# Output projections and norms of a two-layer block, channel-major instead of token-major

## The chip, the cores and the metric

The kernel runs on one core of one Trainium2 chip, written for its engines directly: TensorE (PE), VectorE (DVE), ScalarE (ACT), GpSimd (POOL) and the queue of SyncE (SP), each with its own instruction stream, tied by semaphores. The time is the device time of one execution in microseconds (us), the median of several.

## What is computed

All in fp32, 256 tokens of 2048 channels. A RWKV-7 mixer, a differential attention and a third block with pooling, convolution, gates and an MLP follow one another. What matters here are the three places where an output projection is normed, and the last one after the MLP:

```python
# after the RWKV mixer and after attention (w_out is 2048 x 2048)
x = layernorm(ALPHA * x + (y * silu(g)) @ w_out, ln_g[layer], ln_b[layer])
k_sh, v_sh = x @ w_k_shared, x @ w_v_shared          # after layer 0
# the third block; 16 meta rows stand before the 256 tokens
u = rms_norm(h, g_pre_mix);  proj = u @ w_in
...
h = h + rms_norm(m @ w_o, g_post_mix)
u = rms_norm(h, g_pre_mlp)
f = square(relu(u @ w_up)) @ w_down
out = h + rms_norm(f, g_post_mlp)
```

In the mixer, `y` is group-normed, a bonus term is added, and the sum is multiplied by the gate: bonus and gate wait in DRAM scratch while the scan runs.

## The kernel before

Every weight matrix goes through the core once, in groups of 512 columns. A group is eight slabs of two 128-row tiles (`wraw`, 128x1024). The queue of SP loads them into a ring of four. ScalarE rounds a slab to fp32r (`whi`, `split_hi`, L294), VectorE forms the rest (`wlo`, `split_lo`, L300), and TensorE makes three products for each pair of operands (`three`: high by high, high by low, low by high). `group_slabs` (L305) runs four slabs ahead of TensorE. A slot of the ring comes free when TensorE has used its slab (`slab_used`), so every engine keeps step with TensorE, one slab in 2.8 us.

There are two forms of a group. `ws_group` (L465) keeps a 128x128 tile of weights and streams the 256 tokens: the result has channels on partitions. `wm_group` (L484) keeps the activations and streams 512 weight columns: the result has tokens on partitions. The activations themselves (`ahi`, `alo`) always have channels on partitions.

The projections `wout`, `bout` and `wo` use `wm_group` (`wm_stage`, L718, for the first), so that a norm over the 2048 channels runs along the free axis. For `wout` and `bout`, `ln_evac` (L1477) adds the residual to each group and takes statistics. After the last group, `ln_sqrt`, `ln_norm` and `ln_dve` norm the four column blocks, multiply by the gain row and add the bias row, both spread over partitions by DMA. Then `turn` (L504) transposes the result back to channel-major on TensorE, four tiles a block, and `turned_hi` and `turned_lo` form `ahi` and `alo` for the next stage. After `bout`, the RMS norm of the third block (`squares`, `rms`, `normed_turned`) stands between LayerNorm and turn. After `wo`: `rms(1)`, `post` (gain and residual), `rms(2)`, `normed_turned`. At the end `rms(3)` and `post` work through four column blocks, and SP stores each.

Before `wout`, the last part of the scan ends with the group norm on VectorE (L1377 to L1397). TensorE turns its result (L714), ScalarE applies gain and bias (L1030), VectorE adds the bonus and multiplies by the gate (L1469, L1471), and both engines form `ahi` and `alo` (L1024, L1465). GpSimd issues the loads of gate and bonus (L425, L426) once the last scan product is done.

The order of the engines' work is written out by hand: each engine's program is one list, and hooks put extra steps after chosen slabs.

## Time and profile before

| | |
|---|---|
| median of 3 runs | 2653.46 us (2651.31 to 2658.47) |
| the profiled execution | 2655.8 us, its span 2654.0 us |
| mean granted TensorE clock | 0.967 of full speed |
| TensorE busy | 2491.5 us, 94% |
| VectorE, ScalarE, GpSimd busy | 1538.5, 1122.6, 190.2 us |
| bytes moved | 431.99 MB, mean 163 GB/s |

The profile is that of one execution. Its span runs from the first to the last instruction. "Idle before" is the time in which the engine stood still ahead of an instruction, and the name behind the arrow is what released it. The granted clock is given as a share of full speed: 1.00 is 2.4 GHz and 0.50 is 1.2 GHz. A matmul's end is modelled, so the distance from one start to the next is the better measure of its cost.

### The profile page before, as it was taken

The numbers are of one execution on the slowest core, as the hardware profiler recorded it, in microseconds if no ns is written. First come the engines' busy times: TensorE is split into PE (matmuls) and PEld (weight loads), VectorE is DVE, ScalarE is ACT, GpSimd is POOL, SyncE is SP. The second block draws the span as 40 slices with busy tenths as digits, with TensorE's granted clock in tenths as the row PEclk, the third lists the DMA queues.
The fourth block names the chain that finished last, engine by engine and source line by source line (L and its number), as shares of the span: only waits on it lengthen the run. The fifth ranks groups of instructions, "written<-read, shape, count | busy, mean of one in ns | idle before, by whom it ended". The sixth has DMA issues, their size and how long they took to land.

```text
span 2654.0 us, 51395 instructions
## 1 busy us (share of the span) xinstructions
PE 2491.5 (94%) x21592; PEld 2313.9 (87%) x21592; DVE 1538.5 (58%) x1671; ACT 1122.6 (42%) x1339; POOL 190.2 (7%) x148
## 2 busy tenths in 40 slices
PE   6889999999897999999879999999699999999997
PEld 4889998999787989998679999998599988999885
DVE  6687756654655444555657987555555544455444
ACT  3444343222334444665344434544444433444433
POOL 4053303420000000000000000000000000000000
PEclk8889999999898999999989999999799999999999
DMA  6346563230465665446555656565366666666653
GB/s 188 128 140 210 165 196 110 81 97 28 160 189 161 187 186 179 143 144 185 165 157 174 180 167 175 158 183 173 118 183 183 188 186 188 185 187 182 187 187 126
DMA packets 219285, 431.99 MB, mean 163 GB/s; under 512 B 17057, under 2 KB 21153, under 8 KB 217361
## 3 DMA queue, kind: packets, MB, share of 16 engines
q1 hardware_dynamic: 214496, 404.64, 50.9%
q0 software_dynamic: 3456, 20.51, 2.0%
q10 hardware_dynamic: 1152, 4.19, 0.4%
q8 instruction: 142, 2.33, 0.4%
q14 instruction: 39, 0.31, 0.0%
HBM read 420.91 MB, written 8.39 MB: 162 GB/s over the span
## 4 chain that ended last, share of the span: by engine, by line
PE 85%; DVE 7%; ACT 3%; POOL 2%; DMA 1%; issue 1%; SPq 0%; ACTq 0%; DVEq 0%; POOLq 0%
PE ps L459 25%; PE ps L460 25%; PE ps L461 25%; PE ps L613 6%; DVE wlo L302 2%; ACT whi L298 1%; POOL M L383 1%; POOL M L385 1%; DVE act_lo L1274 1%; PE ps L663 1%; DMA M<-gate_input_scratch 1%; DMA regions<-bonus_scratch 1%; DVE regions L1512 0%; PE ps L512 0%; DVE regions L1745 0%
## 5 line engine op out<-in xcount | busy, mean ns | idle before, releaser
L302 DVE TENSOR_TENSOR wlo<-wraw,whi 128x1024 fp32r<-128x1024 f32 x752 | 953.2, 1272 | 935.9 <-ACT whi L298 934.8
L298 ACT ACTIVATE whi<-wraw 128x1024 fp32r<-128x1024 f32 x752 | 794.9, 1059 | 1255.9 <-PE ps L461 1249.8
L459 PE MATMUL ps<-act_hi,whi 128*128 128x256 f32 (+1 forms) x3968 | 1137.5, 287 | 14.2 <-DVE wlo L302 6.4
L460 PE MATMUL ps<-act_lo,whi 128*128 128x256 f32 (+1 forms) x3968 | 1124.5, 283 | 0.0
L461 PE MATMUL ps<-act_hi,wlo 128*128 128x256 f32 (+1 forms) x3968 | 1122.9, 283 | 0.0
L459 PEld LDWEIGHTS ps<-act_hi,whi 128*128 128x128 f32 x3968 | 755.0, 190 | 19.5 <-DVE wlo L302 7.3
L460 PEld LDWEIGHTS ps<-act_lo,whi 128*128 128x128 f32 x3968 | 757.2, 191 | 0.6
L461 PEld LDWEIGHTS ps<-act_hi,wlo 128*128 128x128 f32 x3968 | 754.3, 190 | 0.0
L459 PE MATMUL ps<-whi,act_hi 128*128 128x512 f32 x512 | 205.2, 401 | 7.4 <-DVE act_lo L1598 7.4
L460 PE MATMUL ps<-wlo,act_hi 128*128 128x512 f32 x512 | 204.7, 400 | 0.0
L461 PE MATMUL ps<-whi,act_lo 128*128 128x512 f32 x512 | 203.3, 397 | 0.0
L461 PE MATMUL ps<-whi,regions_r 128*128 128x512 f32 x512 | 203.0, 396 | 0.0
L460 PE MATMUL ps<-wlo,regions_r 128*128 128x512 f32 x512 | 203.0, 396 | 0.0
L459 PE MATMUL ps<-whi,regions_r 128*128 128x512 f32 x512 | 203.0, 396 | 0.0
L459 PEld LDWEIGHTS ps<-whi,act_hi 128*128 128x128 f32 x512 | 97.4, 190 | 31.9 <-issue 7.7
L461 PEld LDWEIGHTS ps<-whi,act_lo 128*128 128x128 f32 x512 | 97.3, 190 | 23.9
L460 PEld LDWEIGHTS ps<-wlo,act_hi 128*128 128x128 f32 x512 | 97.5, 190 | 22.6
L461 PEld LDWEIGHTS ps<-whi,regions_r 128*128 128x128 f32 x512 | 96.4, 188 | 23.5
L460 PEld LDWEIGHTS ps<-wlo,regions_r 128*128 128x128 f32 x512 | 96.4, 188 | 23.4
L459 PEld LDWEIGHTS ps<-whi,regions_r 128*128 128x128 f32 x512 | 96.4, 188 | 23.4
L613 PE MATMUL ps<-regions 64*64 64x64 f32 x3072 | 103.7, 223 | 8.6 <-POOL regions L418 8.6
L613 PEld LDWEIGHTS ps<-regions 64*64 64x64 f32 x3072 | 97.2, 138 | 15.2 <-POOL regions L418 9.8
(241 smaller groups left out, 1724.9 us busy)
## 6 DMA issues: line engine op xcount, KB each, us to landing
wraw<-in_a_w_in SPq DMA_DIRECT2D x128, 512.0 KB, 4.7
wraw<-in_w_up SPq DMA_DIRECT2D x128, 512.0 KB, 3.7
wraw<-in_w_down SPq DMA_DIRECT2D x128, 512.0 KB, 4.6
wraw<-in_w_in SPq DMA_DIRECT2D x112, 512.0 KB, 3.7
wraw<-in_b_w_qg SPq DMA_DIRECT2D x64, 512.0 KB, 3.9
wraw<-in_a_w_out SPq DMA_DIRECT2D x32, 512.0 KB, 4.6
wraw<-in_w_k_shared SPq DMA_DIRECT2D x32, 512.0 KB, 4.6
wraw<-in_w_v_shared SPq DMA_DIRECT2D x32, 512.0 KB, 4.7
```

The lines of the kernel that those rows point to most:

```text
L298: nc.scalar.activation(whi[:, q % RING], wraw[:, q % RING], ACT.Copy).then_inc(hi_ready, 1)
L302: nc.vector.tensor_tensor(wlo[:, q % RING], wraw[:, q % RING], whi[:, q % RING].bitcast(F32), ALU.subtract).then_inc(lo_ready, 1)
L383: ptt(xtmp(u), xx[:, k2, :], ve(mu)[:, k2].unsqueeze(2).broadcast_to([P, 2, T]), ALU.mult).then_inc(S["xa_mul"], 1)
L385: ptt(xtmp(u), xtmp(u), xT[:, k2, :], ALU.add).then_inc(done, 1)
L459: mm(o, hi_s, hi_m, start=first, stop=False, skip_group_check=True)
L460: mm(o, hi_s, lo_m, start=False, stop=False, skip_group_check=True)
L461: i = mm(o, lo_s, hi_m, start=False, stop=last, skip_group_check=True)
L613: m_ = mm(ps[r_, o_bank, (j % 8) * N:(j % 8 + 1) * N], lhs(r_, j), rhs(r_, j), start=n_ == 0, stop=n_ == len(terms) - 1)
L663: m_ = mm(ps[hs:hs + N, b, (j % 4) * P:(j % 4 + 1) * P].rearrange("p (a t) -> p a t", a=2), Kc[hs:hs + N, j, ts], KR[hs:hs + N, j, :, ts], ...
L1274: st.do(tt(alo[:, k2, 0:T], xtmp(u), ahi[:, k2, 0:T].bitcast(F32), ALU.subtract), sig["xs_ready"])
```

## The change

The three output projections are computed with `ws_group`, channel-major, and their norms too. Sums over channels are now sums over partitions and tiles: VectorE folds the tiles of a group by adds, and products with a vector of ones finish the sum. A scale for each token is spread over the partitions as a product of ones with a diagonal matrix. The transposes ahead of the next stage go away.

- `wout`, `bout`: the first three groups are summed to a preliminary mean, which is taken off before squaring. The last group (`last_group`) is finished tile by tile, and each tile is added, squared and summed behind the next. The normed result comes in seven chunks of 1, 1, 2, 2, 2, 4 and 4 tiles of 128 channels (`norm_dve`, `norm_act`), each chunk released to TensorE when its low part is formed. In `norm_dve`'s list "x" scales and shifts a chunk, "l" forms its low part, and "s" is `split_lo` of a slab. `square_quad` waits until the fold of the square before has begun.
- After `bout`: gain and bias of LayerNorm and of the RMS norm are combined. The RMS scale itself is deferred. The first two `cv` groups use the operand without it and their results are scaled later; the third uses the scaled operand, formed beside the second.
- `wo`: gains are applied at the evacuation, and `H` is kept as it is. The second norm is deferred past the MLP: squared ReLU makes its scale a factor on the MLP's result, which goes into the last norm (`q4`). The residual is completed beside the groups of `up0`, turned to token-major there (32 transposes), and stored from `Htok`.
- The gate and bonus loads are split in 12 (`EARLY`) and 4 tiles of 16. The first part is issued after the sixth state product.
- At the end gain, scale and residual are one operation for each half block, and the stores are issued from SP and ScalarE.
- A square root of a constant is placed where it makes ScalarE load that function's table early.

The core of the diff:

```diff
+CHUNKS = ((0, 1), (1, 2), (2, 4), (4, 6), (6, 8), (8, 12), (12, 16))
 # GpSimd
-            pool.wait_ge(S["y_mm"], 8)
...
-            pool.dma_start(gT, gate_dram[:, :, :]).then_inc(S["gate_loaded"], 16)
-            pool.dma_start(bvT, bonus_dram[:, :, :]).then_inc(S["bv_loaded"], 16)
+            for part, (k0, k1) in enumerate(((0, EARLY), (EARLY, KT))):
+                if part == 0:
+                    pool.wait_ge(S["m_mm"], 6)
+                else:
+                    pool.wait_ge(S["y_mm"], 8)
+                pool.dma_start(bonus_at[part], bonus_dram[:, k0:k1, :]).then_inc(S[f"bv_loaded{part}"], 16)
+                pool.dma_start(gate_at[part], gate_dram[:, k0:k1, :]).then_inc(S[f"gate_loaded{part}"], 16)
+            pool.dma_start(xre, xT_ap[:, :, 1:T + 1]).then_inc(S["x_reloaded"], 16)
 # TensorE
-            wm_stage("wout", lambda k: XS["z"] + k // 2 + 1)
-            turn(0, XS["ln0"], H)
+            def last_group(G, xh, xl, hook, after):
+                outs = [ps[:, b, 0:T] for b in (2, 3, 6, 7)]
+                ws_group(G, [(o, True) for o in outs], T, xh, xl, hook=hook, slabs=SLABS - 2)
+                for b in range(4):
+                    for q in (SLABS - 2, SLABS - 1):
+                        for kk in range(2):
+                            three(outs[b], whi[:, q % RING, kk, c], wlo[:, q % RING, kk, c], xh[:, 2 * q + kk, 0:T],
+                                  xl[:, 2 * q + kk, 0:T], first=False, last=done,
+                                  sig=slab_used if b == 3 and kk == 1 else S["tile_mm"] if done else None)
+                    after(b)
+            def token_sums(i, centred):
+                def tile(n):
+                    if centred:
+                        pe.wait_ge(S["d_ready"], 4 * i + n + 1)
+                        for tb in range(2):
+                            mm(ps[:, 0, tb:tb + 1], block(H[:, 12 + n, :], tb), one, start=n + tb == 0, stop=n == 3, skip_group_check=True)
+                    pe.wait_ge(S["sq1_ready"], 4 * i + n + 1)
+                    for tb in range(2):
+                        mm(ps[:, 5, 2 + tb:3 + tb], block(sq1[n], tb), one, start=False, stop=n == 3, skip_group_check=True)
+                def after(b):
+                    if b == 1:
+                        pe.wait_ge(S["accq_ready"], (1, 2, 4)[i])
+                        for tb in range(2):
+                            mm(ps[:, 5, 2 + tb:3 + tb], block(accQ, tb), one, start=tb == 0, stop=False, skip_group_check=True)
+                    if b:
+                        tile(b - 1)
+                    if b == 3:
+                        tile(3)
+            def spread(i, terms):
+                for a_, term in enumerate(terms):
+                    pe.wait_ge(S["stat_dve"], BY_DVE[f"{term}{i}"])
+                    for tb in range(2):
+                        mm(block(ps[:, SPREAD[a_], :], tb), ones, dg[:, tb, a_, :], start=True, stop=True)
+            for s in range(3):
+                ws_group(G0["wout"] + s, packed(2 * (s % 2)), T, ahi, alo, (lambda k: XS["z"] + k // 2 + 1) if s == 0 else None,
+                         lnv_turn if s == 1 else None)
+            last_group(G0["wout"] + 3, ahi, alo, mean_of(0), token_sums(0, True))
+            spread(0, ("scale", "shift"))
 # ScalarE
+            def mean_hook(i):
+                def hook(u):
+                    if u == 0:
+                        act.wait_ge(S["stat_mm"], MM[f"mean{i}"])
+                        st.do(a(cmean, ps[:, 4, 0:T], ACT.Copy, scale=1.0 / (12 * P)), sig["stat_act"])
+                    if u in (1, 2, 3):
+                        act.wait_ge(S["stat_dve"], BY_DVE[f"cen{i}_{u - 1}"])
+                        square_quad(H[:, 4 * u - 4:4 * u, :])
+            def norm_act(i, nxt, affine, src_, tiles_done):
...
+                for c, (k0, k1) in enumerate(CHUNKS):
+                    act.wait_ge(S["xh_ready"], (XH["ln0"], XH["u1"], XH["u2"])[i] + c + 1)
+                    for k in range(k0, k1):
+                        if affine:
+                            affine(k)
+                    st.do(a(ahi[:, k0:k1, 0:T], src_[:, k0:k1, :], ACT.Copy), sig["n_hi"])
+                    if c >= 3:
+                        split_hi(act, nxt, c + 1)
 # VectorE
+            def add_residual(i, name, other, extra=None):
...
+                def hook(u):
+                    if u == 0:
+                        dve.wait_ge(S["stat_act"], BY_ACT[f"mean{i}"])
+                        st.do(stt(H[:, 12:16, :], other[:, 12:16, :], ALPHA, cmean.unsqueeze(1).broadcast_to([P, 4, T]), ALU.mult, ALU.subtract))
+                    if u < 3:
+                        st.do(tt(H[:, j4, :], H[:, j4, :], cmean.unsqueeze(1).broadcast_to([P, 4, T]), ALU.subtract), sig["stat_dve"])
+                    if u in (2, 3, 4):
+                        fold_squares(u - 2, 3)
+                group_slabs(dve, split_lo, G0[name] + 3, hook, slabs=6)
+                for n in range(4):
...
+                    st.do(tt(H[:, 12 + n, :], H[:, 12 + n, :], last_at[n], ALU.add), sig["d_ready"])
...
+            def norm_dve(i, nxt, scale_chunk, src_):
+                for what, n in (("x", 0), ("x", 1), ("l", 0), ("x", 2), ("l", 1), ("x", 3), ("l", 2), ("s", 2), ("l", 3), ("x", 4),
+                                ("s", 3), ("x", 5), ("l", 4), ("s", 4), ("x", 6), ("l", 5), ("s", 5), ("l", 6), ("s", 6), ("s", 7)):
...
+            for s in range(3):
+                group_slabs(dve, split_lo, G0["cv"] + s, lambda u, s=s: rms_dve(8 * s + u), start=0 if s else 4)
...
+            for c in range(4):
+                for tb in range(2):
+                    st.do(stt(Htok[:, tb, cols], yG[c][:, tb, :], rrstd[:, tb:tb + 1], Htok[:, tb, cols], ALU.mult, ALU.add), sig["out_cols"])
```

## Rows read from the trace of the kernel before

**Rows 1.** The page, part 1: busy us of each engine, share, instructions.
```profile
PE 2491.5 (94%) x21592; PEld 2313.9 (87%) x21592; DVE 1538.5 (58%) x1671; ACT 1122.6 (42%) x1339; POOL 190.2 (7%) x148
```

**Rows 2.** Waits of TensorE: line, releaser: total us, times, longest us.
```profile
PE ps L512 <- DVE regions L1631: 46.5, 6, 20.1
```

**Rows 3.** Windows: busy (x) PE, PEld, DVE, ACT, POOL; granted clock; DMA share, GB/s.
```profile
699.07:706.72 7.65, 0.00 (x1) 0.03 (x1) 3.07 (x5) 1.69 (x4) 0.00 (x0) 0.72 1.00 419
...
801.20:822.26 21.06, 7.52 (x32) 6.32 (x33) 17.54 (x20) 9.93 (x13) 2.67 (x5) 0.59 0.23 79
...
1316.30:1347.28 30.98, 6.39 (x33) 5.76 (x33) 23.43 (x30) 16.05 (x30) 1.98 (x3) 0.62 0.40 137
...
1882.60:1911.69 29.09, 7.26 (x32) 6.46 (x33) 20.92 (x28) 13.96 (x28) 0.54 (x1) 0.57 0.14 40
...
2636.90:2654.00 17.10, 0.00 (x0) 0.00 (x0) 11.82 (x15) 1.74 (x5) 0.00 (x0) 0.63 0.33 123
```

**Rows 4.** Timeline, 670 to 711: start us, us, engine, line, operation, count [idle <-releaser].
```profile
670.61 0.69 DVE L1452 TENSOR_TENSOR M<-M,ps 128x512 f32<-128x512 f32 x1 [3.25 <-PE ps L613]
...
689.24 0.58 POOL L425 DMA_DIRECT2D regions<-gate_scratch  x1 [113.98 <-PE ps L613]
...
691.34 7.73 PE L714 MATMUL ps<-cst,regions 64*64 64x64 f32 x192 [2.40 <-DVE regions L1397]
...
695.17 0.69 DVE L1397 TENSOR_TENSOR regions<-regions,small 128x512 f32<-128x512 f32 x1
...
703.58 0.69 DVE L1469 TENSOR_TENSOR regions<-regions 128x512 f32<-128x512 f32 x1 [7.72 <-DMA regions<-bonus_scratch]
...
706.72 3.68 PE L714 MATMUL ps<-cst,regions 64*64 64x64 f32 x64 [7.66 <-ACT regions L1030]
...
710.33 0.79 PE L459 MATMUL ps<-whi,act_hi 128*128 128x512 f32 x1
```

**Rows 5.** Windows, as rows 3: long and short products, starts after a pause.
```profile
710.32:801.20 90.88, 90.87 (x386) 72.81 (x384) 53.50 (x54) 38.35 (x42) 0.00 (x0) 0.99 0.56 177
...
822.25:825.39 3.14, 3.14 (x16) 3.14 (x15) 1.23 (x1) 1.03 (x1) 0.00 (x0) 0.50 0.89 363
...
1219.07:1222.76 3.69, 0.00 (x1) 0.03 (x1) 2.51 (x3) 3.58 (x4) 0.00 (x0) 0.81 0.55 157
...
1222.76:1228.10 5.34, 5.34 (x13) 4.18 (x14) 4.56 (x4) 3.68 (x4) 0.00 (x0) 0.50 0.31 96
...
2274.80:2456.76 181.96, 181.96 (x1537) 181.95 (x1536) 95.48 (x79) 80.88 (x78) 0.00 (x0) 1.00 0.63 184
```

**Rows 6.** Timeline of TensorE: small products and transposes, columns as rows 4.
```profile
128.48 1.94 PE L546 MATMUL ps<-cst,regions 128*128 128x2 f32 x16
...
1342.07 1.09 PE L512 MATMUL ps<-cst,regions 128*128 128x128 f32 x8 [1.99 <-DVE regions L1631]
...
1647.79 3.61 PE L825 MATMUL ps<-regions,cst 128*128 128x256 f32 x16
```

**Rows 7.** Groups by line and shape: count, busy us, mean ns, idle before.
```profile
L298 ACT ACTIVATE whi<-wraw 128x1024 fp32r<-128x1024 f32 x752 | 794.9, 1059 | 1255.9 <-PE ps L461 1249.8 <-DMA wraw<-in_a_w_in 6.1
...
L1493 DVE TENSOR_TENSOR act_lo<-ps,act_hi 128x1024 fp32r<-128x1024 f32 x12 | 14.7, 1221 | 10.2 <-ACT act_hi L1051 10.2
...
L1030 ACT ACTIVATE regions<-ps,vec 128x256 f32<-128x256 f32 x16 | 8.0, 555 | 0.0
...
L1566 DVE TENSOR_SCALAR regions<-regions,small 128x128 f32<-128x128 f32 x8 | 2.2, 279 | 0.0
```

**Rows 8.** Timeline: a 256-column pass and a table load, columns as rows 4.
```profile
1315.79 0.42 DVE L1615 TENSOR_TENSOR act_lo<-regions,act_hi 128x256 fp32r<-128x256 f32 x1
...
1885.97 1.28 ACT L1157 ACT_TABLE_LOAD   x1
```

**Rows 9.** Timeline of VectorE at the end, columns as rows 4.
```profile
2640.38 1.41 DVE L1745 SCALAR_TENSOR_TENSOR regions<-regions,small 128x512 f32<-128x512 f32 x2
...
2649.57 1.22 DVE L1747 TENSOR_TENSOR regions<-regions 128x1024 f32<-128x1024 f32 x1
```

More of the change, by code:

```diff
@@ L303, in split_lo, with group_slabs @@
                                     ALU.subtract).then_inc(lo_ready, 1)
-        def group_slabs(eng, split, G, hook=None, slabs=SLABS):
-            for u in range(slabs):
+        def group_slabs(eng, split, G, hook=None, slabs=SLABS, start=0):
+            for u in range(start, slabs):
                 g, q = (G, RING + u) if u < RING else (G + 1, u - RING)
@@ L517, in _ @@
+            by_chunk = lambda name: lambda k: XS[name] + chunk_of[k] + 1
             for i in range(2):
@@ new lines, in centred_tile, with tile, lnv_copy @@
+            def centred_tile(i):
+                def tile(n):
+                    act.wait_ge(S["d_ready"], 4 * i + n + 1)
+                    st.do(a(sq1[n], H[:, 12 + n, :], ACT.Square), sig["sq1_ready"])
+                return tile
+            def lnv_copy(u):
+                if u == 5:
+                    act.wait_ge(S["stat_mm"], MM["rows"])
+                    st.do(a(lnv[:, 0:80], ps[:, 6, 0:80], ACT.Copy), sig["stat_act"])
+            for s in range(3):
+                group_slabs(act, split_hi, G0["wout"] + s, lnv_copy if s == 1 else None)
@@ L1770, in _ @@
                         G = G0[f"down{half}"] + 2 * s + part
-                        group_slabs(dve, split_lo, G)
+                        group_slabs(dve, split_lo, G, gained(s - 1) if half and s and part else None)
                     dve.wait_ge(slab_used, SLABS * (G + 1))
```

616 lines of the change are left out of this document (402 added, 214 removed).

## Prediction

> **What bounds the kernel now.** I read the page's busy shares first: TensorE is busy 94% of the span, every other engine at most 58% [rows 1]. So the time is TensorE's products plus the places where TensorE waits, and a change can only pay where it waits, or cost where it lengthens its stream. Second, the list of waits for TensorE: its largest entry, 46.5 us, is the transposes at L512 waiting for VectorE [rows 2]; they stand behind each output projection. Third, the windows laid over the stretches without projection products: 7.65 us before the last turn of the scan's output, 21.06 us after `wout`, 30.98 us after `bout`, 29.09 us after `wo`, 17.10 us at the end [rows 3], 105.9 us together. The reader should see in them that VectorE and ScalarE take turns (17.5 and 9.9 us of the 21.06) while TensorE does only 32 transposes, and that the clock is at half: the first 16 products after the `wout` gap took 3.14 us where 1536 took 181.96, 0.118 each [rows 3, 5]. That start costs 3.14 - 15 x 0.118 = 1.4 us more, here and after `bout`; about 1.1 after `wo`.
>
> **Early bonus and gate loads.** VectorE ends the group norm at 695.86 and starts the output stage at 703.58, held by the load from the scratch; TensorE stands still until 706.72 and starts `wout` at 710.33 [rows 4]. The change issues three quarters of both loads after the sixth state product, seen by VectorE at 670.61 [rows 4]. Now 4 MB, issued at 689.24, are in by 703.5, so 3 MB want about 11 us and land near 682, 14 us early; the last quarter, issued where all was before, is wanted six steps of 1.9 us later. So VectorE starts at 695.9, 7.7 us earlier. TensorE's two last turns no longer follow a pause: at their earlier pace (7.73 us for six) they take 2.6 instead of 3.6 us, from 699.1, and `wout` starts at 701.7, 8.6 us earlier. The slow start of `wout` (six products at 0.43 instead of 0.233) goes too: 1.2 us. Sum 9.8; without the two clock effects 7.7.
>
> **Twelve groups turned round.** Groups of `wout`, `bout` and `wo` had 96 products of 512 columns, now 192 of 256. By the rows 384 long ones take 90.88 us, 1.2 of them the slow start, so 0.2335 each and 22.4 us a group; 1536 short ones take 0.1185 each and 22.75 us a group [rows 5]. Twelve groups cost +4.3 us. The Trainium skill speaks against this edit too: TensorE: Matmul & The Clock Gate, Back-to-back issue gap, gives each product its columns at the clock plus a fixed 2.5 ns, so twice as many products cost more. By that rule the twelve groups would cost an estimated 2.9 us instead of 4.3 and the total would be 1.4 us lower; the row decides.
>
> **New small products inside the stream.** Eight products with a two-column operand left 16 records and took 1.8 us, 0.22 each; eight fp32 products of 256 columns 3.5 us, 0.43 each; eight transposes 1.09 us [rows 6]. Added: two sums for the mean (0.9), the turn of the gain rows (0.15), the deferred RMS scale inside `cv` (two sums, two spreads, 0.9), one residual sum (0.4), 32 transposes inside `up0` (4.4). Sum +6.7 us, all on TensorE, nothing hides it. The 96 old transposes lie inside the windows above.
>
> **LayerNorm after `wout`.** I lay out the last group from its start, with these prices: 1.22 us for 1024 columns on VectorE, 0.69 for 512, 0.42 for 256, 0.28 for a 128-column scaling, 1.06 for a weight rounding and 0.55 for a 256-column scaling on ScalarE [rows 4, 7, 8]. The three old evacuations become adds and folds, hidden beside TensorE's 22.7 us. Sum for the mean at 5.7, `cmean` at 6.6. Then the queues of both engines hold one another: a square (ScalarE) waits until the fold before it has begun (VectorE), the next weight rounding stands behind that square, and VectorE's `wlo` behind that rounding. VectorE: add and first centring to 9.0, third centring 13.7, fold 14.4; ScalarE square to 15.4, rounding 16.5; `wlo` 17.7, fold 19.1; square 19.5, rounding 20.6, `wlo` 21.8, fold 23.7, `wlo` 24.9, first tile added 25.3. TensorE is through tile 1 at 20.3 and must wait for the folded squares (23.7) and the first tile (25.3); then sums 0.9, tile 2, sums, tile 3: 30.0 at full clock. So 6.9 us more than a plain group (22.66 plus 0.43 counted above). Idle of 3.69 us was followed by 5.34 us at half clock [rows 5]; the same here slows 24 products and the sums: +3.
> Tail: tile 4 added 30.5, squared 30.9, sums 31.75, variance 31.95, root 32.2, reciprocal 32.4, diagonal 33.0, spread 33.75, second diagonal and spread 34.5, first chunk scaled and shifted 34.95, gain 35.55, rounded 36.0, low part 36.45: TensorE resumes 6.45 us after its last tile.
> First `ks` group: VectorE owes per four k three passes of 1.22 and two `wlo`, 6.1 us, where TensorE wants 5.7. Walking the written order of chunks (1, 1, 2, 2, 2, 4, 4) gives TensorE stalls of 0.3, 0.7, 1.8 and 1.9 us: 4.7. A slow start is absorbed by the third.
> Before: 21.1 + 1.4 = 22.4. After: 6.9 + 3 + 6.45 + 4.7 = 21. Gain 1.4 us.
>
> **LayerNorm and RMS norm after `bout`.** The same new chain, stalls 4.0 since a `cv` product has 272 columns: 20.4. Before 31.0 + 1.4 = 32.4, because a second norm stood in line. It is now deferred: squares, folds and the scale run beside the first two `cv` groups, and the third group needs the scaled operand. VectorE and ScalarE spend about 3.1 to 3.7 us a slab there against TensorE's 3.0, and four slabs of ring cover it; cover gone, each slab costs 0.7. Gain 12.0 us.
>
> **RMS norms after `wo`.** No centring: squares and folds are done a group ahead. Inline cost 1.3 (two sums for the folds and for three tiles); tail: square 0.45, sum 0.45, root 0.35 (its table is loaded early, which hides 1.28 us [rows 8]), reciprocal and diagonal 0.75, spread 0.5, scale and add 0.95, rounding and low part 0.85, hand-overs: 4.65; stalls in the first `up0` group 4.6. Sum 10.6 against 29.1 + 1.1. Gain 19.5 us. VectorE's new residual work (two passes of 1.22 in four slots) puts it behind the second `up0` group: -0.5.
>
> **The end.** Before: last product 2636.9, VectorE's evacuation, ScalarE's two squares, root by 2640.4, then four rounds of 2.6 us to 2650.8 and 3.2 us for the last store [rows 9]. After: the gain product hides under the squares; two more tiny scalings (+0.4), then eight fused passes at 0.67: 5.4 instead of 10.4 us. Gain 4.7 us. The stores are half as large and split over two queues; I count nothing for that.
>
> **Sum.** 9.8 + 1.4 + 12.0 + 19.5 + 4.7 = 47.4, less 4.3 + 6.7 + 0.5 = 11.5: 36 us gained. The profiled execution took 2655.8 us, 1.8 of them around its span of 2654.0, and lies 2.3 above the median of 2653.46; it becomes 2619.8, and against the median 2617.5.
>
> **Bounds of what the trace does not show.** The half clock inside the last group: 0 to 4.5 us a norm. The weave's wait there: between 0 (if the squares' turn is not the one that comes last) and 10 (each of three hand-overs a further 1.1). The chunked first groups: 0 to 9 us each, for VectorE's share is within 8% of TensorE's. I take my walk through the code for each, since every step has a row.
>
> **Rivals.**
> *Leaner tails (chance 0.15).* If the engines run ahead where I let them wait, the last groups lose neither 6.9 nor the clock's 3 in two norms: 2 x 9.9 less, 2598. For: the ring holds four slabs, so a late `wlo` need not be felt. Against: the written order puts squares before roundings in one queue.
> *Dearer weave (0.16).* The hand-overs cost double in two last groups and in three first groups: +6.9 and +3 x 3.5, 2635. For: VectorE owes 6.1 us where TensorE wants 5.7. Against: short operations follow one another within 0.04 us in the rows.
> *The early loads do not help (0.04).* If another wait lies right behind the load (ScalarE's first write), 7.7 us are lost: 2625. The rows show ScalarE's write done 7 us before, so it is unlikely.
> *Slower than before (0.05): the chunk sweep runs in lockstep.* Some 20 VectorE steps a sweep each wait for a ScalarE step and that for VectorE. TensorE starves for the delay of each, in three sweeps. The 36 us are gone at 0.6 us a step; at 0.85 a step (a rounding of 512 columns and its hand-over) it costs 51 us: 2669. Against: in the written order two chunks of scaling stand between a chunk and its low part.
>
> **How the numbers follow.** The forecast case, 2617.5, has 0.60 and its own range is 2607 to 2629. With both neighbours in, 2598 to 2638 leaves out some 2 in 10. A measurement of this kernel tells about 0.3% from no change, 8 us, so "faster" is below 2645.5. Forecast, leaner, loads and nearly all of the dearer case lie there: 0.92; same 0.04, from the dearer case's end; slower 0.04.
>
> **What would show it.** Right: `wout` starts near 702; between the last `wout` product and the first of `ks` some 6.5 us, not 21; a hole of about 5 us inside that last group, ended by VectorE; holes of 1.8 and 1.9 us at the seventh and ninth k of `ks`, `cv` and `up0`; no hole in the second `cv` group; 12.4 us after the last product instead of 17.1. Wrong: many holes near 1 us in the first groups (lockstep), half clock for long stretches of them, or a wait for the RMS scale in `cv`.

## The result, and the profile after

The changed kernel takes 2632.33 us (median of 5 runs, 2629.56 to 2641.17) against 2654.44 of the kernel before on the same chip: ratio 0.9918, 95% interval 0.9897 to 0.9939. That is faster by more than 0.3%, 22 us by the medians. The profiled execution took 2629.58 us, its span is 2627.8; the spans differ by 26.2 us (2654.0 before). The forecast was 2617.5 with a gain of 36 us, so the time is 15 us above the forecast: inside the wide range of 2598 to 2638, but above 2607 to 2629, the range given for the forecast case by itself, and nearest to the 2635 of "dearer weave".

First the page, part 1 (as [rows 1]), then the waits of TensorE (as [rows 2]) from the last group of `wout` on (769 to 830) and from that of `bout` on (1280 to 1400). L492 is the first product of a triple, L574 the sum of the folded squares, L594 a spread, L894 the RMS sum in the second `cv` group.

```profile
PE 2504.4 (95%) x22809; PEld 2380.5 (91%) x22809; DVE 1576.8 (60%) x1756; ACT 1166.1 (44%) x1433; POOL 191.0 (7%) x149
```

```profile
PE ps L492 <- DVE act_lo L1756: 4.5, 3, 2.1
PE ps L574 <- DVE regions L1692: 2.9, 1, 2.9
PE ps L594 <- DVE M L1744: 1.3, 1, 1.3
```

```profile
PE ps L894 <- DVE regions L1692: 5.2, 1, 5.2
PE ps L492 <- DVE act_lo L1756: 3.5, 2, 2.1
PE ps L574 <- DVE regions L1692: 3.3, 1, 3.3
PE ps L594 <- DVE M L1744: 1.3, 1, 1.3
```

The 46.5 us at the turns are gone. What the reader is to see in their place is L1692: it is the last step of the fold of squares, and three holes of TensorE wait for it, 2.9, 3.3 and 5.2 us. For each of the first two a hole of "about 5 us" was forecast, for the third none: "no hole in the second `cv` group", and a wait there was named as a sign of being wrong.

The windows that answer to [rows 3] (columns as there): behind the last tile of `wout`, `bout` and `wo`, and behind the last product.

```profile
803.97:812.70 8.73, 5.29 (x26) 4.93 (x24) 4.27 (x16) 4.19 (x8) 1.66 (x3) 0.50 0.15 53
1320.34:1326.77 6.43, 2.97 (x24) 2.66 (x24) 4.26 (x16) 4.19 (x8) 0.00 (x0) 0.87 0.00 0
1876.14:1881.70 5.56, 2.17 (x13) 1.73 (x12) 2.73 (x9) 3.73 (x7) 0.00 (x0) 0.68 0.00 0
2615.02:2627.79 12.77, 0.00 (x0) 0.00 (x0) 8.48 (x14) 1.74 (x5) 0.00 (x0) 0.65 0.49 164
```

They were 21.06, 30.98, 29.09 and 17.10 us [rows 3]: 98.2 together, now 33.5. So 65 us of gaps went, and 26 us of time. The rest came back inside the stream, as turned groups, small products and new holes. The table says what each stretch gained. It goes by the first product of each stage in the trace's records (before: scan's last product ends 688.94, `wout` 710.33, `ks` 822.26, `vs` 914.71, `bout` 1222.76, `cv` 1347.28, gates 1493.08, `wo` 1791.31, `up0` 1911.69, `down0` 2094.89, last product ends 2636.85, after: 688.39, 701.22, 812.70, 908.33, 1216.38, 1326.77, 1483.56, 1782.09, 1881.70, 2073.05, 2615.02). The forecast is put together from the terms of the prediction for the same stretch; small products and turned groups are in it.

| stretch | before | after | gained | forecast |
|---|---|---|---|---|
| scan's end to `wout` | 21.39 | 12.83 | 8.6 | 8.6 |
| `wout` and `ks` | 204.38 | 207.11 | -2.7 | +0.6 |
| `bout`, `cv` and pool | 270.32 | 267.18 | 3.1 | 9.2 |
| `wo` and `up0` | 303.58 | 290.96 | 12.6 | 12.8 |
| the end | 17.15 | 12.78 | 4.4 | 4.7 |

The rest (start to the scan's end, `vs` to `bout`, gates to `wo`, `down0` on) gives 0.2. Three of five stretches came out within 0.3 us. The missing 9.4 us lie in two: 3.3 in `wout` and `ks`, 6.1 in `bout`, `cv` and pool.

In both, one thing is late. ScalarE in the last group of `wout` (start, duration, engine, line, operation, operands, count, idle before and its releaser); L1176 squares four tiles, L328 rounds weights:

```profile
779.33 1.06 ACT L1176 ACTIVATE regions<-regions 128x1024 f32<-128x1024 f32 x1 [1.48 <-DVE regions L1722]
780.29 1.04 ACT L328 ACTIVATE whi<-wraw 128x1024 fp32r<-128x1024 f32 x1
784.53 1.06 ACT L1176 ACTIVATE regions<-regions 128x1024 f32<-128x1024 f32 x1 [3.19 <-DVE regions L1686]
785.50 1.04 ACT L328 ACTIVATE whi<-wraw 128x1024 fp32r<-128x1024 f32 x1
788.49 1.06 ACT L1176 ACTIVATE regions<-regions 128x1024 f32<-128x1024 f32 x1 [1.95 <-DVE regions L1686]
```

The squares wait 3.19 and 1.95 us for L1686, the first step of a fold, which empties the one buffer of squares. The rounding of weights stands behind them in the queue, and VectorE waits for that (2.13 and 1.41 us ahead of its `wlo` at 786.57 and 790.54). In the first `cv` group the same ring runs, first ScalarE, then VectorE:

```profile
1352.03 2.08 ACT L1323 ACTIVATE regions<-regions,lnv 128x256 f32<-128x256 f32 x4 [1.90 <-DVE regions L1686]
1354.02 1.04 ACT L328 ACTIVATE whi<-wraw 128x1024 fp32r<-128x1024 f32 x1
1356.95 2.08 ACT L1323 ACTIVATE regions<-regions,lnv 128x256 f32<-128x256 f32 x4 [1.90 <-DVE regions L1686]
```

```profile
1355.09 1.23 DVE L332 TENSOR_TENSOR wlo<-wraw,whi 128x1024 fp32r<-128x1024 f32 x1 [3.10 <-ACT whi L328]
1356.23 0.68 DVE L1686 TENSOR_TENSOR regions<-regions 128x512 f32<-128x512 f32 x1
```

Squares 2.08, rounding 1.04, `wlo` 1.23, fold 0.68: a round takes 1356.95 - 1352.03 = 4.92 us (the steps overlap by some 0.1), in which ScalarE idles 1.90 and VectorE 2.4 to 3.4. Neither is short of time; they hand one buffer back and forth. That is the theory that the experiments test. Its rivals: VectorE's own load is what is late; TensorE merely asks too early; the ring of four weight slabs runs dry.

### The profile page after: what moved, and what is told of

Same layout as the page of the kernel before. It is cut to its first block, busy times and chain, and to the rows that moved or that the text cites. A ratio compares the mean times of both kernels' runs of the same rounds, so it can differ in the third digit from the quotient of the medians.

```text
span 2627.8 us, 53992 instructions
## 1 busy us (share of the span) xinstructions
PE 2504.4 (95%) x22809; PEld 2380.5 (91%) x22809; DVE 1576.8 (60%) x1756; ACT 1166.1 (44%) x1433; POOL 191.0 (7%) x149
## 4 chain that ended last, share of the span: by engine, by line
PE 81%; DVE 11%; ACT 4%; issue 2%; POOL 1%; DMA 1%; SPq 0%; DVEq 0%; ACTq 0%; POOLq 0%
PE ps L492 24%; PE ps L493 23%; PE ps L494 23%; PE ps L695 6%; DVE wlo L332 4%; ACT whi L328 2%; DVE act_lo L1476 1%; PE ps L745 1%; PE ps L603 1%; DMA M<-gate_input_scratch 0%; DVE act_lo L1756 0%; DVE regions L1489 0%; POOL M L419 0%; PE ps L845 0%; DVE regions L1686 0%
## 5 line engine op out<-in xcount | busy, mean ns | idle before, releaser
L492 PE MATMUL ps<-act_hi,whi 128*128 128x256 f32 (+1 forms) x4736 | 1360.3, 287 | 35.0 <-DVE act_lo L1867 12.7
L493 PE MATMUL ps<-act_lo,whi 128*128 128x256 f32 (+1 forms) x4736 | 1343.9, 284 | 0.0
L494 PE MATMUL ps<-act_hi,wlo 128*128 128x256 f32 (+1 forms) x4736 | 1342.1, 283 | 0.0
L328 ACT ACTIVATE whi<-wraw 128x1024 fp32r<-128x1024 f32 x752 | 793.1, 1059 | 1145.5 <-PE ps L494 1127.5
L492 PEld LDWEIGHTS ps<-act_hi,whi 128*128 128x128 f32 x4736 | 903.3, 191 | 43.2 <-issue 27.8
L493 PEld LDWEIGHTS ps<-act_lo,whi 128*128 128x128 f32 x4736 | 906.3, 191 | 0.6
L494 PEld LDWEIGHTS ps<-act_hi,wlo 128*128 128x128 f32 x4736 | 902.8, 191 | 0.0
L492 PE MATMUL ps<-whi,regions_r 128*128 128x512 f32 x512 | 203.0, 396 | 0.0
L492 PEld LDWEIGHTS ps<-whi,regions_r 128*128 128x128 f32 x512 | 96.4, 188 | 23.4
L1933 DVE SCALAR_TENSOR_TENSOR regions<-regions,vec 128x256 f32<-128x256 f32 x240 | 100.1, 478 | 0.0
L454 POOL TENSOR_TENSOR regions<-regions,cst 128x512 f32<-128x512 f32 x48 | 68.1, 1439 | 113.1 <-DVE regions L1611 56.9
L421 POOL TENSOR_TENSOR M<-M,regions 128x512 f32<-128x512 f32 x32 | 54.9, 1714 | 2.5
L493 PE MATMUL ps<-wlo,act_hi 128*128 128x512 f32 x128 | 50.7, 396 | 0.0
```

The source lines that it names most:

```text
L328: nc.scalar.activation(whi[:, q % RING], wraw[:, q % RING], ACT.Copy).then_inc(hi_ready, 1)
L421: ptt(xtmp(u), xtmp(u), xT[:, k2, :], ALU.add).then_inc(done, 1)
L454: ptt(Bm[:, fs].rearrange("p (h t) -> p h t", h=8), AB[:, fs].rearrange("p (h t) -> p h t", h=8), cs(f"level{lv}").unsqueeze(1).broadcast_ ...
L492: mm(o, hi_s, hi_m, start=first, stop=False, skip_group_check=True)
L493: mm(o, hi_s, lo_m, start=False, stop=False, skip_group_check=True)
L494: i = mm(o, lo_s, hi_m, start=False, stop=last, skip_group_check=True)
```

## Experiments

Medians and ratios are against the kernel before on the same chip in the same call.

| kernel | median us | ratio | 95% interval | span |
|---|---|---|---|---|
| changed kernel | 2632.3 | 0.9918 | 0.9897 to 0.9939 | 2627.8 |
| late_loads | 2642.3 | 0.9954 | 0.9937 to 0.9970 | 2641.2 |
| two_bufs_cv | 2620.7 | 0.9878 | 0.9862 to 0.9895 | 2619.1 |
| two_bufs_all | 2609.4 | 0.9830 | 0.9813 to 0.9847 | 2606.7 |
| wait_later | 2634.6 | 0.9928 | 0.9912 to 0.9945 | 2630.5 |
| sums_last | 2624.5 | 0.9892 | 0.9873 to 0.9912 | 2620.6 |
| filled | 2608.3 | 0.9827 | 0.9813 to 0.9842 | 2606.6 |
| bonus_early | 2609.7 | 0.9834 | 0.9816 to 0.9851 | 2608.2 |
| no_shift | 2604.5 | 0.9816 | 0.9797 to 0.9835 | 2602.8 |
| gate_split | 2608.2 | 0.9827 | 0.9812 to 0.9842 | 2606.4 |

Single executions differ by a few us upstream of anything changed: the same wait of TensorE, 2.17 us in the scan, ends at 597.38 us in the changed kernel and at 601.40 in late_loads. So each verdict rests on the stretch concerned. two_bufs_all adds to two_bufs_cv, filled and bonus_early add to two_bufs_all, no_shift and gate_split add to filled, and the others change the changed kernel by itself. no_shift leaves out an addition that the result needs.

### Two buffers in the first `cv` group

```
+        sqb = [sqq, r6(2048, 1024)]
-                    act.wait_ge(S["sq_free"], quads[0])
+                    act.wait_ge(S["sq_free"], max(6, quads[0] - 1))
-                        st.do(a(sqq[:, (k % 4) * T:...
+                        st.do(a(sqb[t % 2][:, (k % 4) * T:...
-                    fold_squares(t - 5, 4)
+                    fold_squares(t - 5, 4, sqb[(t - 5) % 2])
```

> The changed kernel with two buffers in turn for the four quads of RMS squares in the first cv group, nothing else. Theory (one buffer makes a ring of squares 2.08, rounding 1.06, residue 1.22 and first fold 0.69 us: rounds of 4.93 us instead of 3.1): the rounds fall to about 3.1 to 3.2 us, which is ScalarE's own work, the sum of squares is ready 5 us earlier, the hole of 5.15 us at 1363.96 and the half clock behind it (2.3 us) are gone: 6.5 to 7.5 us shorter, a span of about 2620.5. Rival (VectorE is what is late: its folds stand behind the residues of weights): the rounds stay near 4.9 us and the time within 1 us of the changed kernel. Rival (the ring of four slabs runs dry anyway, since 3.1 us a slab is above TensorE's 3.0): the hole moves and keeps over 2 us.

ScalarE in the same place (the edit moves lines by one):

```profile
1349.54 2.07 ACT L1324 ACTIVATE regions<-regions,lnv 128x256 f32<-128x256 f32 x4
1351.56 1.06 ACT L329 ACTIVATE whi<-wraw 128x1024 fp32r<-128x1024 f32 x1
1352.53 2.07 ACT L1324 ACTIVATE regions<-regions,lnv 128x256 f32<-128x256 f32 x4
1354.58 1.06 ACT L329 ACTIVATE whi<-wraw 128x1024 fp32r<-128x1024 f32 x1
1355.54 2.06 ACT L1324 ACTIVATE regions<-regions,lnv 128x256 f32<-128x256 f32 x4
```

Rounds of 3.0 us without idle time, and of the waits between 1340 and 1400 only these are left:

```profile
PE ps L493 <- DVE act_lo L1757: 1.5, 1, 1.5
PE ps L493 <- DVE act_lo L1904: 0.4, 1, 0.4
```

The hole of 5.2 us is gone and the half clock at 1366.1 with it; `cv` and pool take 149.66 us instead of 156.79, 7.1 us less. The theory holds in size too. VectorE does the same work as before, so its load is out, and so is a dry ring as the cause. That the span is 8.7 us shorter, as forecast, is in part chance: the last group and tail of `wout`, which this edit leaves alone, took 4.8 us less in this execution and `bout` 2.6 more.

### Two buffers in the last groups of `wout` and `bout` as well

```
-                        square_quad(H[:, 4 * u - 4:4 * u, :])
+                        square_quad(H[:, 4 * u - 4:4 * u, :], sqb[(u - 1) % 2], max(3 * i, quads[0] - 1))
-                        fold_squares(u - 2, 3)
+                        fold_squares(u - 2, 3, sqb[(u - 2) % 2])
```

> As the one before, with two buffers in turn also for the three quads of squares in the last groups of wout and bout. Theory (in those groups ScalarE waited 3.19 and 1.95 us for the first fold before its second and third quad, and VectorE then 2.13 and 1.41 us for the rounded weights behind them, and so accQ was late): the holes of 2.94 us at 790.66 and 3.31 us at 1308.21 are gone or under 0.5 us, with a part of the half clock behind them (some 2 us in the two tails): 6 to 8 us shorter than with two buffers in cv alone, a span of about 2613.5. Rival (TensorE waits there because VectorE's own work in the last group, 12 subtractions and adds of 1.22 us among the residues, fills the time): each hole keeps over 2 us, and the span is within 2 us of the kernel with two buffers in cv.

Waits of TensorE from the last group of `wout` to the start of `ks` (L595 the spread, L563 the column sums of a tile), and below them the windows of the last group, the tail and the `ks` stage, first of the changed kernel, then of this one (columns as [rows 3]; the third number from the end is the granted clock):

```profile
PE ps L595 <- DVE M L1746: 1.3, 1, 1.3
PE ps L563 <- DVE regions L1733: 0.3, 1, 0.3
```

```profile
769.78:803.97 34.19, 30.64 (x218) 30.09 (x216) 20.75 (x27) 11.59 (x14) 0.00 (x0) 0.83 0.39 127
...
812.70:908.33 95.63, 93.23 (x768) 92.87 (x769) 52.81 (x49) 47.02 (x54) 0.00 (x0) 0.98 0.55 175
```

```profile
769.37:795.84 26.47, 26.00 (x219) 25.66 (x217) 20.57 (x27) 11.72 (x14) 0.00 (x0) 1.00 0.51 165
795.84:803.05 7.21, 3.75 (x23) 3.40 (x24) 4.27 (x16) 4.19 (x8) 1.65 (x3) 0.71 0.20 64
803.05:898.67 95.62, 93.95 (x769) 93.78 (x769) 52.82 (x49) 47.13 (x54) 0.00 (x0) 0.97 0.54 175
```

The last group falls from 34.19 to 26.47 us, with VectorE and ScalarE as busy as before (20.75 and 20.57, 11.59 and 11.72). Of the 7.7 us, 2.9 are the hole and 4.8, by subtraction, what the half clock made of the products and sums behind it (0.83 against 1.00). That is the upper end, for the changed kernel's execution has the longest half clock of all: against two_bufs_cv, last group and tail are 4.5 us shorter, `bout` 7.0, together 11.5 of the 12.4 us between the two spans. The tail falls by 1.5 for the same reason. In `bout` (its first product to the first of `cv`) 105.93 us against 110.39 to 115.45 in the four kernels that have one buffer and the sums between the tiles. I had expected 6 to 8 us and the span fell by 12.4: the two holes are 6.2 of it, and I priced too little of the clock behind them. With this, the kernel is 1.7% faster than the one before, where the change alone gave 0.8%.

### The wait for the RMS sum two slabs later

```
-                if q == 2:
+                if q == 4:
                     pe.wait_ge(acc_act, ACC_ACT["cv"] + 1)
                     pe.wait_ge(S["accq_ready"], 3)
```

and every later step of the norm two slabs later, also the one that forms the scaled operand (and VectorE waits for its own last step once more ahead of the first gate).

> The changed kernel with one buffer as it is, but the sum of the RMS squares and all that follows from it two slabs later in the second cv group (TensorE's wait for it after slab 5 of the group instead of slab 3). Theory (TensorE is held by its wait for the sum, and not for want of weights): the rounds stay at 4.93 us, the hole of 5.15 us is gone or under 1 us, and so is the half clock behind it: 5 to 7.5 us shorter than the changed kernel, a span of 2620.5 to 2623. Rival (the slow rounds drain the ring of four slabs, the wait for the sum only comes to stand in front of that): TensorE waits 3 to 5 us for a slab instead, and the span is within 2 us of the changed kernel's 2627.8. Rival (the later steps collide with the third group): a new hole after slab 1 of the third group, where the scaled input is first needed.

```profile
1377.82:1384.28 6.46, 0.01 (x2) 0.04 (x1) 4.24 (x4) 3.25 (x4) 0.00 (x0) 0.86 0.43 114
1324.17:1486.26 162.09, 151.74 (x1161) 150.77 (x1162) 126.18 (x179) 87.56 (x116) 0.00 (x0) 0.96 0.52 156
```

```profile
1364.64 0.39 PE L492 MATMUL ps<-act_hi,whi 128*128 128x272 f32 x1 [0.27 <-DVE wlo L332]
...
1384.28 0.56 PE L492 MATMUL ps<-act_hi,whi 128*128 128x272 f32 x1 [6.45 <-DVE act_lo L1903]
```

The first half of the theory held: TensorE went past the place where it had stood (37.2 us into `cv`, 1361.4 here) and on to 1377.8, five slabs more, with one pause of 0.27 us for a slab. So the ring of slabs was all but dry under the slow rounds, yet not what held TensorE: that was its wait for the sum. The gain did not come, and the last of the rivals did: the third group then waited 6.45 us for its scaled operand (L1903), which the edit itself makes two slabs later, and `cv` and pool took 162.1 us, 5.3 more. Asking later helps only where nothing else stands on the result. The sum has to come earlier, which the second buffer does.

### All sums after the last tile

```
+                    if centred and b < 3:
+                        return
-                    if b == 1:
+                    if b == (3 if centred else 1):
...
-                        tile(b - 1)
+                        for n in (range(3) if centred else (b - 1,)):
+                            tile(n)
```

> The changed kernel with its one buffer, but in the last groups of wout and bout TensorE takes every sum (the folded squares and all four tiles) after the fourth tile, and none between the tiles: only the place of TensorE's wait is moved, no engine's work. Theory (the sum of folded squares is late because one buffer holds it back; the place of the wait decides how much of that TensorE loses): the sum is needed 3 tiles of 1.4 us later and has come by then, so the holes of 2.94 and 3.31 us are gone, and the tails are longer by the small products that stood between the tiles (10 of them, some 1.1 to 2.3 us by the clock): 1 to 4 us shorter than the changed kernel for both stages together. Rival (VectorE adds the tiles one after the other and is behind by the same time, so the tile sums wait in place of the fold's): the sum of holes in each last group and its tail stays within 1 us of the changed kernel's.

Tails of `wout` and `bout`, sums now among them:

```profile
795.21:808.96 13.75, 9.37 (x44) 8.93 (x45) 6.33 (x21) 5.18 (x11) 1.65 (x3) 0.57 0.32 104
1307.57:1319.27 11.70, 6.94 (x46) 6.51 (x45) 6.71 (x21) 5.18 (x11) 0.00 (x0) 0.71 0.28 88
```

The holes in the two groups are gone (0.5 us at L576 is what is left), the tails are 5.0 and 5.3 us longer than in the changed kernel, where 1.1 to 2.3 were expected: they hold the sums, and half clock with them (0.57 and 0.71). Last group and tail of `wout` take 37.50 us; the four kernels with one buffer and the wait between the tiles took 38.2 to 42.9, so the place of the wait is worth 0.7 to 5.4 us, the upper end with the longest half clock. Two buffers take 33.68. `bout` up to the first product of `cv` takes 106.6 us, 105.9 with two buffers and 110.4 to 115.5 with one and the sums between the tiles. The rival is out: the tiles' sums did not wait in the fold's place (0.9 us a norm). For the last groups this is the second-best cure, and of a different kind: it moves the wait, it doesn't shorten the ring.

### Tails filled with products

```
+            filler(5)
             spread(0, ("scale", "shift"))
+            filler(8)
```

where `filler(n)` is n products of `ones` by the identity into a free bank; the same around the second spread. The kernel under it is the one with two buffers everywhere.

> The kernel with two buffers everywhere, and in the tails behind the last groups of wout and bout 13 products of ones by the identity (128 columns, results not used) for TensorE: 5 ahead of its wait for the scale, 8 behind the spreads, that is in its holes of 1.31 and 2.15 us. Theory (the half clock of 10.2 us at 798.8 and at 1307.4 follows the idle TensorE of the tail, and what it costs is what the same products take at full clock less: 8 spread products at 0.236 instead of 0.118, some 27 triples of the next group at 0.64 instead of 0.36 us): the granted clock stays 1.0 through both tails, 3 to 4 us saved at each, a span of 2599 to 2601. Rival (the clock falls there whatever TensorE does, or the added products come late into the way of the chain): the clock falls as before and each tail is 0 to 1 us longer, a span of 2606 to 2609.

Tail of `wout`, `ks` stage, tail of `bout`:

```profile
797.30:803.74 6.44, 5.99 (x51) 5.57 (x50) 4.27 (x16) 4.19 (x8) 1.65 (x3) 1.00 0.26 71
803.74:899.38 95.64, 91.98 (x768) 91.28 (x769) 52.82 (x49) 46.92 (x54) 0.00 (x0) 1.00 0.54 176
1306.52:1312.95 6.43, 5.98 (x49) 5.56 (x50) 4.27 (x16) 4.19 (x8) 0.00 (x0) 1.00 0.00 0
```

The clock stayed at its upper level (1.00, 2.4 GHz) through both tails, as the theory said, and only 0.8 us came of it in the tail of `wout` (7.21 to 6.44). The expected 3 to 4 us a norm did not: the `ks` stage took 95.64 us at full clock and 95.62 with half clock at its start. TensorE is faster by 2 us there (91.98 busy against 93.95) and waits 2 us longer. So in the first group behind a norm the slow start costs nothing; something else sets the pace. The span, 2606.6 us, is what the rival had forecast, though its mechanism is not what happened.

### Without the shift in the chunk sweep

```
-                    st.do(tt(x_, x_, over(0, k0, k1), ALU.mult))
+                    st.do(tt(x_, x_, over(0, k0, k1), ALU.mult), sig["xh_ready"])
...
-                    st.do(tt(x_, x_, over(1, k0, k1), ALU.add), sig["xh_ready"])
```

This is done to the kernel with filled tails, and in both LayerNorms.

> The kernel with two buffers and filled tails, with one part left out: VectorE doesn't add the shift row to the chunks of the two LayerNorms (the spread of it is still made). With filled tails the clock stayed at 1.0, yet the ks stage took 95.64 us as before it did with half clock (95.62), and the holes of the first ks group grew to 0.60, 1.39 and 1.67 us. Theory (the first group behind a LayerNorm is bound by VectorE's sweep: for four tiles of 128 columns 1.22 scale, 1.22 shift, 1.22 low part and two times 1.22 for the low parts of the weights, 6.1 us against 5.7 us of products, on top of its slow start): without the shift VectorE has 4.9 us, the holes are gone but for a start of under 1 us, the ks stage falls by 3 to 4.5 us to 91 to 92.5 and the cv and pool stages by 2.5 to 4 us, and each tail by 0.4 us. Rival (ScalarE is as late: affine 2.08, high part 1.06 and two roundings of 1.06, 5.25 us, started behind it): the holes keep over 2 us in the ks stage, which stays above 94.

`ks` stage, then `cv` and pool, then the tail of `bout`:

```profile
804.07:896.27 92.20, 91.51 (x771) 91.16 (x770) 48.33 (x44) 46.52 (x54) 0.00 (x0) 1.00 0.56 182
1314.27:1460.01 145.74, 145.29 (x1163) 145.10 (x1162) 120.50 (x172) 85.44 (x114) 0.00 (x0) 1.00 0.58 174
1304.57:1314.27 9.70, 9.70 (x52) 9.70 (x50) 4.58 (x16) 5.19 (x10) 0.00 (x0) 0.54 0.00 1
```

TensorE's waits around the `ks` stage, with filled tails and then without the shift:

```profile
PE ps L493 <- DVE act_lo L1767: 4.0, 4, 1.7
```

```profile
PE ps L493 <- DVE act_lo L1767: 0.7, 1, 0.7
```

One VectorE pass fewer, and `ks` falls by 3.4 us and `cv` and pool from 149.74 to 145.74. TensorE's waits are 0.7 us instead of 4.0. So VectorE's sweep bounds the first groups behind a norm, ScalarE doesn't, and 3.4 and 4.0 us are what this one pass of it costs. The third row is a warning: here the clock had fallen before the tail (half from 1299.9 to 1313.6), and the tail, with TensorE busy throughout on sums, spreads and the 13 added products, took 9.70 us instead of 6.43. At half clock without added products the tail of `wout` in the changed kernel took 8.73.

### Early loads undone

```
-                if part == 0:
-                    pool.wait_ge(S["m_mm"], 6)
-                else:
-                    pool.wait_ge(S["y_mm"], 8)
+                pool.wait_ge(S["y_mm"], 8)
```

> The changed kernel with one part undone: the loads of bonus and gate for the first twelve tiles again wait for the scan's last outputs (y_mm 8) instead of its sixth state. Theory (the early loads are worth what the trace shows between the last scan product and the first product of wout: 12.8 us in the changed kernel against 21.4 before, and 1.2 us of slow first products): about 9 us longer than the changed kernel, a span of about 2636.5, and the stretch between the two products back at about 21 us. The hole of 1.33 us before L695 in the scan's last round is charged by this theory to the transfers that now run beside the scan: it is gone here, so that the loss is 8.5 to 9 net. Rival (the stretch is bound by the group norm or by VectorE and the gain came from somewhere else): less than 4 us longer, span under 2632. Rival on the hole (not the transfers, something of the profile's own): the hole at about 680 us is still there.

```profile
703.62 0.69 DVE L1669 TENSOR_TENSOR regions<-regions 128x512 f32<-128x512 f32 x1 [4.83 <-DMA regions<-gate_scratch]
```

```profile
695.39 0.69 DVE L1672 TENSOR_TENSOR regions<-regions 128x512 f32<-128x512 f32 x1
```

The first row is of this kernel, the second of the changed one, where VectorE goes from the group norm into the output stage without a wait. Scan's end to `wout` takes 19.01 us, 12.83 with early loads, 21.39 before. I had expected about 21 again. So the early start is worth 6.2 us of the 8.6; the other 2.4 are put down to the split, since with 3 MB instead of 4 to land VectorE waits 4.83 us and not 7.72 [rows 4]. The medians say 10 us for the early start, but of the spans' 13.4 us 4.0 lie ahead of the scan's last round, and `bout` took 5.1 us more in this execution. The hole in the scan's last round is not there.

### What makes the hole in the scan's last round

TensorE of the changed kernel (here "issue": nothing that the profile shows):

```profile
681.16 1.43 PE L695 MATMUL ps<-work,regions 64*64 64x64 f32 x41 [1.33 <-issue]
```

Bonus alone early:

```
                 pool.dma_start(bonus_at[part], ...
+                if part == 0:
+                    pool.wait_ge(S["y_mm"], 8)
                 pool.dma_start(gate_at[part], ...
```

> The kernel with two buffers everywhere, in which only the bonus is loaded early and the gate of the first twelve tiles waits for the scan's last outputs again. In the changed kernel the 3 MB of early transfers end at 680.8 us, and TensorE's sequencer stands 1.33 us in the scan's last round, where a packet of the queue of instructions begins at 678.9 us, 1.9 us later in its round than in the kernel with late loads. Theory (that packet stood behind the early transfers): these are half as long and end before the packet's time, the hole before the scan's products at 679 is gone, 1.3 to 1.5 us gained there; and VectorE then waits 2 to 4 us for the gate ahead of wout, since 1.5 MB by itself came 8.1 us after its issue against 6.6 us that VectorE needs for the group norm: in all 0.5 to 3 us longer than the kernel with two buffers everywhere. Rival (the hole is the profile's or the code's own and not the transfers'): the hole stays at 1.3 to 1.5 us.

Bonus and a third of the gate early:

```
+                    pool.dma_start(gate_at[0][:, 0:4, :], ...).then_inc(S["gate_loaded0"], 16)
+                    pool.wait_ge(S["y_mm"], 8)
+                    pool.dma_start(gate_at[0][:, 4:EARLY, :], ...).then_inc(S["gate_loaded2"], 16)
```

> The kernel with two buffers and filled tails, in which only the bonus of twelve tiles and the gate of the first four are loaded early (2 MB instead of 3), the gate of the next eight after the scan's last outputs. Theory (the hole in the scan's last round comes when a packet of instructions stands behind early transfers; 2 MB end some 3.5 us sooner, and VectorE needs the next eight tiles of gate not before some 699 us): no hole at 680 us (1.3 to 1.5 us gained) and no wait for a load in the output stage: 1 to 1.5 us shorter than the kernel with filled tails, a span of about 2605. Rival (the late 1 MB, behind nothing on its queue but landing some 7 us after 689, is needed at once): a VectorE wait of 0.5 to 2 us in the output stage, and the same time.

Busy share of the DMA engines in 40 slices of 0.4 us, from 668 to 684 us, of the changed kernel and of bonus_early:

```profile
DMA  0000010936999989999999799995120000010000
```

```profile
DMA  0100000000200919958989973120000000020000
```

In the first the transfers keep the engines busy up to 678.8 and the last packets end at 680.0, in the second the share falls from 677.2 on and only single packets come after. A packet of 16 KB on the queue of instructions begins 3.65 us after TensorE's restart in this round in the changed kernel (675.23, 678.88), 3.70 in filled; 1.30 in late_loads, 1.07 in bonus_early and 1.59 in gate_split. In the first two TensorE's sequencer stands 1.33 and 1.47 us, in the other three not at all. In the changed kernel, filled and gate_split the packet begins about as the early transfers thin out. Both expectations held: bonus_early is 1.2 us faster to the scan's end and waits 2.06 us for the gate, 2.0 lost (14.63 us to `wout` instead of 12.64). gate_split has neither hole nor wait: 1.4 us less from the scan's earlier hole to its end (89.99 against 91.36 us). Its median equals that of filled within 0.2 us, and its span too, since 1.9 us were lost upstream; 1.4 us is below what these runs can tell. That a transfer delays the packet is shown by three kernels that moved or cut the transfer; which stage of the queues it waits in isn't. Nor is the second hole of this kind explained: in the turn ahead of `wout` TensorE stands 1.31 us for "issue" before 697.92 in the changed kernel, and 0.2 to 1.9 us in the others, late_loads (0.45) among them. The kernel before has none there.

## The prediction, point by point

- **Early loads: right.** 8.56 us instead of 8.6 at the start of `wout` (701.22; forecast 701.7), and the slow start is gone (clock 1.00 from 693.7), which was priced at 1.2. By late_loads 6.2 of the 8.6 are the early start itself. Missed: the hole of 1.33 us that the transfers make in the scan.
- **Turned groups: right.** The three undisturbed groups of `wout` take 68.56 us (701.22 to 769.78) with the turn of the gain rows in them, 22.8 each, forecast 22.75. By the rule of the Trainium skill (TensorE: Matmul & The Clock Gate, Back-to-back issue gap), 2.5 ns for each of 96 more products on top of the 22.4 of the old groups, an estimated 22.64 would have been due. The trace is nearer to the row's price.
- **Small products: right in sum.** The 32 transposes took 3.5 us where I said 4.4, the residual sum and the hole behind the second `up0` group 0.4 and 0.9 where I said 0.4 and 0.5.
- **LayerNorm after `wout`: the mechanism right, one term mis-sized.** The walk is what the trace shows, in its order: squares behind folds, roundings behind squares, TensorE stopped by the folded squares. They were ready 23.8 us into the group and the first tile 25.2, forecast 23.7 and 25.3. The hole of 5 came as 2.9 and 0.5 us with the first sums between, and TensorE came to it 0.6 us late; without the half clock the group would have ended at an estimated 29.4 us (34.19 less the 4.8 below), forecast 30.0. What failed is the term for the clock, "the same here slows 24 products and the sums: +3": 23.9 us at half clock followed (792.7 to 816.6), not 5.34. It cost 4.8 us in the last group and 2.3 in the tail (8.73 against 6.44 at full clock), 7.1 for 3. The tail itself came out at full clock as forecast, 6.45, with 6.44 and 6.43 in filled. The stalls of the first group too: 4.7 forecast, 4.6 measured (95.63 - 4 x 22.75), and "a slow start is absorbed by the third" is what filled shows.
- **After `bout`: the step that failed** is "about 3.1 to 3.7 us a slab there against TensorE's 3.0, and four slabs of ring cover it". I added up each engine's work, and it is right as work: with two buffers the round is 3.0 us. I didn't look at who frees the buffer that the squares are written to, though I had walked that same handshake for the last group one paragraph before. Rounds took 4.92 us, the sum came 5.2 us late and half clock followed: 7.1 us by two_bufs_cv. The sign of being wrong that the prediction named, a wait for the RMS scale in `cv`, is what came. The stretch misses 6.1, since its other terms came out 1 us better (6.8 us of half clock followed the hole in its last group, not the 23.9 of `wout`).
- **`wo`: right, with two errors that cancel.** The tail took 5.56 us, 0.9 more than forecast, the transposes 0.9 less. Against 182.0 plain [rows 5] `up0` takes 9.4 us more; without the 3.5, 0.4 and 0.9 above, 4.6 are left for the stalls, 4.6 forecast. That VectorE's sweep makes them here too is by likeness only; no run took it away in `up0`.
- **The end: right.** From the last product 12.77 us, 12.4 forecast. VectorE's eight fused passes, in place of the four rounds of [rows 9]:

```profile
2618.93 5.39 DVE L2088 SCALAR_TENSOR_TENSOR regions<-regions,small 128x512 f32<-128x512 f32 x8
```

- **The rivals.** "Leaner tails" came about in part with two buffers: 2609 where 2598 was given for it, since the sums between the tiles remain (last group of `wout` 26.47 us, a plain one with the sum for the mean 23.1) and some half clock in the tails. "Dearer weave" has the nearest number, 2635, by luck: its hand-overs did not double, the last groups' holes are smaller than forecast and the first groups cost what I said. What made the kernel dearer is the clock and the ring in `cv`. The lockstep sweep is not there: single holes of 0.7 and 1.7 us, as the walk gave them, and no long row of small ones.

## What to carry over

Where two engines share a single buffer, the time of a round can be the sum of all steps around the ring, not the larger of the two engines' shares. A second buffer made it the latter here (4.92 to 3.0 us), and in three places it was worth as much (23 us by the medians) as the whole restructuring had brought (22). Both engines idle in turn, each with the other's name as releaser, is what such a ring looks like in the profile. Part of this ring is only the written order: the fold stands behind `wlo` in VectorE's list. Whether the fold ahead of `wlo` would shorten the rounds with one buffer was not tried. A late result isn't cured by asking for it later unless nothing else stands on it; and before pricing a slow clock, look whether the stretch is bound by TensorE at all.

## What the runs showed of the hardware

- After a hole of about 3 us in the same place (last group of `wout`, one buffer) the granted clock stood at half (1.2 GHz) for 23.9 us in one execution, and for 10.2, 6.8 and 3.4 us, each with a second stretch of 6.8 in the tail, in three others. Its length couldn't be foretold from the hole; last group and tail of `wout` varied from 38.2 to 42.9 us with it.
- With thirteen products of 128 columns in the idle places the clock stayed at full through both tails in filled and in gate_split, and through the first in no_shift. In no_shift's second, with the same products, it had fallen 4.7 us ahead of the tail of `bout`, behind a hole of 0.71 us which in filled and two_bufs_all had no such effect. Why there and not in the others is open.
- Reads of 3 MB beside a tight stretch of short products went with a late packet of instructions and a hole of 1.3 to 1.5 us. With 1.5 MB, 2 MB or none there was no hole. The profile names it "issue", which looks like nothing at all.
